# Seven rounds of a state-space scan: X and Y turned by VectorE blocks and transfers in place of TensorE, and TensorE's slab wait split in two

## The reference

```python
h = h + 0.5 * _swiglu(_rmsnorm(h, ffn1_norm[l]), ...)
h = h + _mixer(_rmsnorm(h, mix_norm[l]), ...)       # three mixers, gated and summed
h = h + 0.5 * _swiglu(_rmsnorm(h, ffn2_norm[l]), ...)
return _rmsnorm(h, final_norm)
```

```python
xbc = jax.nn.silu(_causal_conv(_in_cols(u, w_in, 6), ssm_conv_w, ssm_conv_b))
xs_, bm, cm = jnp.split(xbc, [SSM_D_INNER, SSM_D_INNER + SSM_GROUPS * SSM_DSTATE], axis=-1)
...
def step(state, inp):
    xc, bc, cc, dtc, dac = inp
    cum = jnp.cumsum(dac, axis=1)
    seg = cum[:, :, None] - cum[:, None, :]
    decay = jnp.exp(jnp.where(mask, seg, -jnp.inf))
    cb = jnp.einsum('btgn,bsgn->btsg', cc, bc)
    xdt = xc * dtc[..., None]
    y = jnp.einsum('btsg,btsgr,bsgrp->btgrp', cb, decay, xdt)
    y = y + jnp.einsum('btgn,bgrpn->btgrp', cc, state) * jnp.exp(cum)[..., None]
    to_end = jnp.exp(cum[:, -1:] - cum)
    state = jnp.exp(cum[:, -1])[..., None, None] * state + jnp.einsum('bsgn,bsgrp->bgrpn', bc, xdt * to_end[..., None])
    return state, y
...
y = y.reshape(bsz, seq, SSM_D_INNER) * jax.nn.silu(z.astype(F32))
y = _rmsnorm(y.reshape(bsz, seq, SSM_GROUPS, SSM_D_INNER // SSM_GROUPS),
             ssm_norm.reshape(SSM_GROUPS, SSM_D_INNER // SSM_GROUPS))
y_ssm = y.reshape(bsz, seq, SSM_D_INNER).astype(u.dtype) @ w_branch_ssm
```

## Time and profile before

| | us |
|---|---|
| median of three runs | 1797.28 |
| the three runs | 1797.56, 1797.28, 1795.0 |
| profiled execution | 1794.89 |
| its span in the trace | 1793.1 |

### The profile page before, as it was taken

How to read it: one execution, slowest core, us unless ns; L and a number is a source line. 1 busy time by engine, 2 the same in 40 slices (tenths; PEclk the granted TensorE clock), 3 DMA queues, 4 the chain that set the end, 5 groups by cost and what they waited for, 6 DMA issues and landing times.

```text
span 1793.1 us, 26524 instructions
## 1 busy us (share of the span) xinstructions
PE 1784.8 (100%) x10012; PEld 1504.1 (84%) x10012; DVE 959.2 (53%) x1393; ACT 633.3 (35%) x1002; POOL 89.0 (5%) x92
## 2 busy tenths in 40 slices
PE   9999999999999999999999999999999999999998
PEld 7888888888888888888988888888888888888887
DVE  5444443369988888623544445665334544444333
ACT  5222322244544445422333344443222332222221
POOL 2111100000000000000000000000000011111000
PEclk9999999999999999999999999999999999999999
DMA  5333323334233332232222323322333332233332
GB/s 172 105 94 100 98 94 105 105 96 94 83 94 88 87 95 84 69 106 94 95 71 71 94 82 93 93 90 74 94 98 99 96 94 94 94 96 102 106 105 71
DMA packets 53937, 169.30 MB, mean 94 GB/s; under 512 B 6336, under 2 KB 13760, under 8 KB 53872
## 3 DMA queue, kind: packets, MB, share of 16 engines
q1 hardware_dynamic: 45824, 159.15, 27.9%
q10 hardware_dynamic: 8048, 9.24, 2.7%
HBM read 166.21 MB, written 2.16 MB: 94 GB/s over the span
## 4 chain that ended last, share of the span: by engine, by line
PE 95%; DVE 3%; ACT 1%; issue 1%; DMA 0%; ACTq 0%; DVEq 0%; SPq 0%
PE G L547 48%; PE I L547 16%; PE G L614 11%; PE G L567 8%; PE I L1050 1%; PE I L1026 1%; PE I L1016 1%; PE G L874 1%; PE I L674 1%; PE I L811 1%; PE I L820 1%; DVE CV L1936 1%; PE I L830 1%; DVE WL L1673 1%; PE I L986 0%
## 5 line engine op out<-in xcount | busy, mean ns | idle before, releaser
L1673 DVE TENSOR_TENSOR WL<-RAW,WH 128x1024 fp32r<-128x1024 f32 x296 | 372.1, 1260 | 290.0 <-ACT WH L1147 280.8
L1147 ACT CAST WH<-RAW 128x1024 fp32r<-128x1024 f32 x295 | 306.4, 1046 | 225.2 <-PE I L547 125.9
L547 PE MATMUL G<-UH,WH 128*128 128x512 f32 x664 | 164.2, 389 | 0.0
L547 PE MATMUL G<-UH,WL 128*128 128x512 f32 x664 | 164.0, 389 | 0.0
L547 PE MATMUL G<-UL,WH 128*128 128x512 f32 x664 | 163.9, 389 | 0.0
L547 PEld LDWEIGHTS G<-UL,WH 128*128 128x128 f32 x664 | 124.6, 188 | 25.9
L547 PEld LDWEIGHTS G<-UH,WL 128*128 128x128 f32 x664 | 124.6, 188 | 25.9
L547 PEld LDWEIGHTS G<-UH,WH 128*128 128x128 f32 x664 | 124.5, 188 | 25.9
L547 PE MATMUL G<-NH,WH 128*128 128x512 f32 x448 | 113.5, 395 | 0.0
L547 PE MATMUL G<-NL,WH 128*128 128x512 f32 x448 | 110.8, 389 | 0.0
L547 PE MATMUL G<-NH,WL 128*128 128x512 f32 x448 | 110.7, 389 | 0.0
(11 more groups left out here) (352 smaller groups left out, 2619.3 us busy)
## 6 DMA issues: line engine op xcount, KB each, us to landing
RAW<-in_slabs SPq DMA_DIRECT2D x296, 512.0 KB, 3.5
cum_rows<-kept_rows ACTq DMA_DIRECT2D x16, 256.0 KB, 6.8
bias<-in_rel ACTq DMA_DIRECT2D x16, 128.0 KB, 2.8
bias<-in_rel ACTq DMA_DIRECT2D x16, 112.0 KB, 2.8
h<-in_x SPq DMA_DIRECT2D x6, 256.0 KB, 5.7
out_y<-h SPq DMA_DIRECT2D x4, 256.0 KB, 2.2
h<-in_x ACTq DMA_DIRECT2D x2, 256.0 KB, 3.6
out_y<-h ACTq DMA_DIRECT2D x4, 128.0 KB, 1.8
```

What stands on the lines that cost most here:

```text
L547: ins = mm(dst, slab(W, n)[:, (k - k0) * P:(k - k0 + 1) * P], R[:, k, :], start=begin and which == 0 and k == k0, stop=end and which == 2 ...
L1147: nc.scalar.copy(slab(WH, n), RAW[:, n.slot, :]).then_inc(split_hi, 1)
L1673: V.tensor_tensor(slab(WL, n), RAW[:, n.slot, :], slab(WH, n).bitcast(F32), ALU.subtract).then_inc(split_lo, 1)
```

## The change

Three things change.

1. X of groups 1 to 7 (`turn_x`, `move_x`): DVE turns the 32 x 32 blocks of XT in place of TensorE (two `transpose` instructions of 128 x 512 float32 each round, put between `lo(n+5)` and silu 2), and SP moves the blocks to their partitions with 16 transfers of 32 partitions x 8 pieces of 128 bytes (32 KB each). ACT's XD and DVE's XTE and XDT then read `x_tokens` in SBUF. Group 0 is still turned by TensorE.
2. Y of groups 0 to 6 (`turn_y`, `move_y`): two more DVE transposes of 128 x 512 behind `ssm_scale`, 16 more transfers in two parts with a slab's load between them. `ssm_hi` and `ssm_lo` read the result from SBUF (SU, which lies where SL lies). `ssm_hi` moves to ACT's t = 3, `ssm_lo` and `group_gain` to the end of DVE's round, and in the stage behind the rounds both move behind `lo(n+5)`. Group 7 is still turned by TensorE.
3. TensorE waits for the rounded slab (`need_hi`) ahead of a slab's first matmul and for its remainder only ahead of the last third. The second state update no longer waits for `ssm_hi` and `ssm_lo`; new waits for `ssm_lo` stand ahead of the products that read SH and SL.

The buffers lie in places that are free at the time. The diff, cut to its core:

```diff
+            def move_x(g):
+                sp.wait_ge(x_blocks, g)
+                for b in range(4):
+                    for q in range(4):
+                        sp.dma_start(x_tokens[32 * q:32 * q + 32, :, :].rearrange("p j (f c) -> p (j f) c", f=2)[:, :, 32 * b:32 * b + 32],
+                                     x_turned[32 * b:32 * b + 32, :, 32 * q:32 * q + 32]).then_inc(x_moved, 16)
...
+            def move_y(g, parts):
+                sp.wait_ge(y_blocks, g + 1)
+                for b in parts:
+                    for q in range(4):
+                        sp.dma_start(SU[32 * q:32 * q + 32, bass.ds(2 * g, 2), :].rearrange("p f (j c) -> p (f j) c", c=P)[:, :, 32 * b:32 * b + 32],
+                                     y_turned[32 * b:32 * b + 32, :, 32 * q:32 * q + 32]).then_inc(y_moved, 16)
...
+            ahead = N_SSM + 15
+            loads(RING, ahead)
+            move_x(1)
+            next_load(At(ahead))
+            move_y(0, (0, 1))
+            next_load(At(ahead + 1))
+            move_y(0, (2, 3))
+            with sp.Fori(0, NG - 2) as i:
+                for j in range(2, 6):
+                    next_load(At(ahead + j, i, 6))
+                move_x(i + 2)
+                next_load(At(ahead + 6, i, 6))
+                move_y(i + 1, (0, 1))
+                next_load(At(ahead + 7, i, 6))
+                move_y(i + 1, (2, 3))
+            loads(ahead + 6 * (NG - 2) + 2, N_SLABS)
...
             def fm(dst, n, RH, RL):
+                need_hi(n)
+                blocks(dst, n, 0, KT, RH, RL, True, False, (0, 1))
                 need_slab(n)
-                blocks(dst, n, 0, KT, RH, RL, True, True).then_inc(slab_done, 1)
+                ins = blocks(dst, n, 0, KT, RH, RL, False, True, (2,))
+                ins.then_inc(slab_done, 1)
...
-                for j in range(TT):
-                    for f in range(2):
-                        nc.tensor.transpose(I01[:, j * 256 + f * P:j * 256 + (f + 1) * P],
-                                            XT[:, f, j * P:(j + 1) * P], ident[:])
+                if isinstance(g, int) and g == 0:
+                    for j in range(TT):
+                        for f in range(2):
+                            nc.tensor.transpose(I01[:, j * 256 + f * P:j * 256 + (f + 1) * P],
+                                                XT[:, f, j * P:(j + 1) * P], ident[:])
...
-                pe.wait_ge(sems["ssm_hi"], last("ssm_hi", g - 1))
-                pe.wait_ge(sems["ssm_lo"], last("ssm_lo", g - 1))
...
-                    0: lambda: (ssm_turn(i), ssm_turn_back(i - 1)), 1: lambda: ssm_cb_u(i),
+                    0: lambda: ssm_turn(i), 1: lambda: ssm_cb_u(i),
...
             ssm_turn(g)
-            ssm_turn_back(g - 1)
+            pe.wait_ge(sems["ssm_lo"], last("ssm_lo", 3))
             output_half(n + 1, wn + 1, 0, (0, 1))
...
             need_slab(n + 4)
+            pe.wait_ge(sems["ssm_lo"], last("ssm_lo", NG - 2))
             output_part(n + 4, wn + 1, KT, 2 * KT - 2, SH, SL, False, False)
...
+            def turn_y(g):
+                dve.wait_ge(sems["ssm_scaled"], last("ssm_scaled", g))
+                dve.wait_ge(sems["ssm_scaled_act"], last("ssm_scaled_act", g))
+                if not isinstance(g, int) or g > 0:
+                    dve.wait_ge(y_moved, 256 * g)
+                for f in range(2):
+                    ins = V.transpose(y_turned[:, TT * f:TT * f + TT, :], Y[:, :, f * P:(f + 1) * P])
+                ins.then_inc(y_blocks, 1)
+            def turn_x(g):
+                dve.wait_ge(sems["conv_done"], after("conv_done", g, 1))
+                dve.wait_ge(x_moved, 256 * (g - 1))
+                dve.wait_ge(sems["x_copied"], after("x_copied", g - 1))
+                for f in range(2):
+                    ins = V.transpose(x_turned.rearrange("p (j f) c -> p f j c", f=2)[:, f, :, :],
+                                      XT[:, f, :].rearrange("p (j c) -> p j c", c=P))
+                ins.then_inc(x_blocks, 1)
...
                     if t == 0 and not first:
                         ssm_x(inner)
-                        ssm_lo(inner - 1)
-                        group_gain(inner)
                     if t != 2 or not first:
                         lo(n + t + 3)
+                    if t == 2:
+                        turn_x(p)
...
                     ssm_scale(inner)
+                turn_y(inner)
                 z_silu(p, wn + 4)
                 lo(n + 7)
                 group_scalars(p)
                 lo(n + 8)
+                if not first:
+                    ssm_lo(inner - 1)
+                    group_gain(inner)
```

More of the change, by code:

```diff
@@ L417, in _, with next_load @@
                 sp.dma_start(wgk_raw[32 * k:32 * k + 16, :], a["wgk"]).then_inc(wgk_landed, 16)
[L418 to L425, removed]
+            def next_load(n):
+                sp.wait_ge(split_lo, n.value - (RING - 1))
+                load(n)
@@ new lines, in move_x, with loads @@
+            def move_x(g):
[4 more added lines that the diff above has]
+                                     x_turned[32 * b:32 * b + 32, :, 32 * q:32 * q + 32]).then_inc(x_moved, 16)
+            def loads(begin, end):
+                whole = -(-begin // RING)
+                for n in range(begin, whole * RING):
+                    next_load(At(n))
+                with sp.Fori(whole, end // RING) as i:
+                    for j in range(RING):
+                        next_load(At(j, i, RING))
+                for n in range(end // RING * RING, end):
+                    next_load(At(n))
@@ L612, in tm_tile @@
                         if j == 0 and which == 0 and k == 4:
+                            need_hi(n + 1)
+                        if j == 0 and which == 2 and k == 0:
+                            need_slab(n)
+                        if j == 0 and which == 2 and k == 4:
                             need_slab(n + 1)
@@ L1925, in ssm_lo, with ssm_lo_last @@
                 dve.wait_ge(sems["group_gain"], after("group_gain", g))
[L1926 removed]
+                dve.wait_ge(y_moved, 256 * (g + 1))
+                for f in range(2):
+                    dve.wait_ge(sems["ssm_hi"], after("ssm_hi", g, f))
+                    inc(V.scalar_tensor_tensor(tile_of(SL, 2 * g + f), tile_of(SU, 2 * g + f), ssm_norm_cols[f],
+                                               tile_of(SH, 2 * g + f).bitcast(F32), ALU.mult, ALU.subtract), "ssm_lo")
+            def ssm_lo_last():
+                dve.wait_ge(sems["group_gain"], after("group_gain", NG - 1))
+                evict_lo(I34, SH, SL, 2 * NG - 2, ssm_norm_cols, "ssm_hi", NG - 1, "ssm_lo")
+            def turn_y(g):
[3 more added lines that the diff above has]
+                    dve.wait_ge(y_moved, 256 * g)
+                for f in range(2):
+                    ins = V.transpose(y_turned[:, TT * f:TT * f + TT, :], Y[:, :, f * P:(f + 1) * P])
+                ins.then_inc(y_blocks, 1)
             taps_n = [0]
@@ L1972, in ssm_x @@
             def ssm_x(g):
-                dve.wait_ge(sems["x_copied"], after("x_copied", g))
-                inc(V.tensor_tensor(XTE[:].rearrange("p j (r c) -> p (j r) c", c=CH), heads(I01[:]), rows(2),
+                if isinstance(g, int) and g == 0:
+                    source = heads(I01[:])
+                    dve.wait_ge(sems["x_copied"], after("x_copied", g))
+                else:
+                    source = x_tokens.rearrange("p j (r c) -> p (j r) c", c=CH)
+                    dve.wait_ge(x_moved, 256 * g)
+                dve.wait_ge(sems["u_done"], last("u_done", g - 1))
+                inc(V.tensor_tensor(XTE[:].rearrange("p j (r c) -> p (j r) c", c=CH), source, rows(2),
                                     ALU.mult), "xte_ready")
                 dve.wait_ge(sems["intra_done"], last("intra_done", g - 1))
-                inc(V.tensor_tensor(XDT[:].rearrange("p j (r c) -> p (j r) c", c=CH), heads(I01[:]), rows(1),
+                inc(V.tensor_tensor(XDT[:].rearrange("p j (r c) -> p (j r) c", c=CH), source, rows(1),
                                     ALU.mult), "xdt_ready")
+            def turn_x(g):
+                dve.wait_ge(sems["conv_done"], after("conv_done", g, 1))
+                dve.wait_ge(x_moved, 256 * (g - 1))
+                dve.wait_ge(sems["x_copied"], after("x_copied", g - 1))
+                for f in range(2):
+                    ins = V.transpose(x_turned.rearrange("p (j f) c -> p f j c", f=2)[:, f, :, :],
+                                      XT[:, f, :].rearrange("p (j c) -> p j c", c=P))
+                ins.then_inc(x_blocks, 1)
             def ssm_cb(g):
@@ L2182, in _ @@
             lo(n + 5)
+            ssm_lo(g - 1)
+            group_gain(g)
             ssm_scale(g)
-            ssm_lo(g)
+            ssm_lo_last()
             lo(n + 6)
```

55 lines of the change are left out of this document (44 added, 11 removed).

## The result

| | before | after |
|---|---|---|
| median, 20 runs each | 1794.91 us (1794.36 to 1797.56) | 1799.09 us (1797.96 to 1799.99) |
| ratio, 95% interval | 1 | 1.0022 (1.0016 to 1.0028) |
| span of the profiled execution | 1793.1 us | 1796.4 us |
| busy PE, DVE | 1784.8, 959.2 us | 1777.4, 976.9 us |
| five looped rounds, `gconv` to `gconv` | 208.48 us | 213.68 us |

The change makes the kernel slower by 4.2 us, just over the 3.6 us that I had called the limit of what can be told. The forecast was -0.7 us. By the spans it is +3.3 us where the sum had -0.7: 4.0 us to explain.

What follows compares the result with a forecast made beforehand. PE bound the rounds at 42.18 us; afterwards DVE's chain would, at 41.91. The update starts 1.4 us earlier, a new wait returns 0.7: net -0.7 us, 1796.6 us against the median of 1797.28; range 1793 to 1806.5.

Steps and rivals of the forecast that it cites:

- PE sets the rounds now, DVE's chain of 40.83 us is next: Looped rounds: PE takes 42.18 us without a gap; the chain of DVE and ACT is only 1.35 us under it.
- Rival (c): DVE's chain has slack read as fixed, so PE sets the rounds again: 1786.4 us, in part 1792; chance 0.12.
- The price of a block transpose, t = 0.60: Each DVE transpose of 512 float32 per partition takes 0.60 us, one element per cycle and lane.
- (a): DVE's transposes are slow: at t = 1.14 the time is 1807.8 us; chance 0.20, mostly nearer 0.9.
- (b): DVE's transposes run at the double rate, t = 0.40: 2.8 us less, 1793.8; chance 0.07.
- `turn_x` in full on the chain, `turn_y` in the wait of `z_silu`: DVE's rounds: turn_x adds 1.20 us in seven rounds; turn_y costs nothing up to t of about 0.88.
- Transfers and split waits cost nothing: SP's moves are hidden up to about 0.85 us an issue; TensorE's two waits per slab win and lose nothing.
- (d): SP's issues exceed 0.85 us or queued loads come late; at 1.0 us an issue +17, 1813 us; chance 0.06.
- (e): Small transfer pieces choke the DMA engines: +56 us in each of seven rounds, near 2190 us; chance 0.02.
- `ssm_lo`, moved behind `lo(n+8)`, stays on the chain: Late in DVE's looped round: the moved passes stay on the chain, with 0.12 us back in each looped round.
- read from SBUF its two passes cost 1.28 against 1.40: ssm_lo on DVE: two passes cost 2 x 0.60 + 0.08 from SBUF against 1.40, 0.12 us back each looped round.
- PE's clock: PE's granted clock stays full if waits of 2.7 us leave it so; a fall would add to the slow side.

Runs made afterwards that it cites:

- Y alone, mended: Changed kernel with X turned by TensorE again, ssm_lo and group_gain moved earlier in loop and stage behind, ssm_hi(6) earlier behind the loop: 1788.61 us, ratio 0.9968.
- X alone: Changed kernel with Y turned by TensorE again and ssm_hi, ssm_lo, group_gain back at their old places; only X moved: 1795.75 us, ratio 1.0004.
- the run of the split waits alone: Kernel before with only the split waits for rounded parts and remainders added: 1794.54 us, ratio 0.9998.
- the mended order: Whole change with ssm_lo and group_gain ahead of group_scalars and lo(n + 8), reordered stage behind, 5 added matmuls a round: 1795.49 us, ratio 1.0003.
- Y alone: Changed kernel with X turned by TensorE again in all rounds; only Y by VectorE's blocks and transfers: 1790.86 us, ratio 0.9978 to before.
- the run with added matmuls: Changed kernel with 5 more unused 128 x 128 matmuls on TensorE each round, ahead of the products of B and C: 1798.17 us, ratio 1.0018 to before.

## Why the prediction was wrong

Its structure held and its sum was short by 4.0 us of span, enough to turn a small gain into a loss. The step that failed is the price of moving `ssm_lo` and `group_gain` to the end of the loop's body: the sum put it at 0.12 us back in each looped round, and the trace shows 0.47 to 0.52 us of new idle time a round, ahead of `gconv`, and nothing back. A second cost, the falls of TensorE's clock, was named and put at nothing.

The forecast's 1796.6 us stand nearer to the measured 1799.09 than the sum deserves. They rest on a median of three, 1797.28; over 20 runs it is 1794.91, from which the same sum gives 1794.2, and the miss is 4.9 us. Two smaller sums don't come out either: by PE's side, 11.6 us less 2.7 + 5 x 1.4 + 1.0 + 0.7 leaves a gain of 0.2 us and not 0.7, and t from 0.53 to 0.72 at 14 us for each microsecond gives 1795.6 to 1798.3. Point by point:

- **PE sets the rounds now, DVE's chain of 40.83 us is next:** right, and seen bare in the 40.84 us of Y alone, mended. Rival (c), slack in that chain, falls.
- **The price of a block transpose, t = 0.60:** right. Two of them, once for X and once for Y:

```profile
442.24 1.30 DVE L2097 STREAM_TRANSPOSE x_turned<-XT 128x512 f32<-128x512 f32 x2
...
539.59 1.30 DVE L2030 STREAM_TRANSPOSE y_turned<-Y 128x512 f32<-128x512 f32 x2 [0.23 <-DVE Y L2153]
```

  A pair is recorded at 1.30 us; in the stream of the chain the next pass starts 1.22 us behind the pair's start (483.91 to 485.13), 0.61 each. Rivals (a) and (b) fall. The Trainium skill (VectorE: DVE Perf Modes, The three transpose paths) gives 311 ns for 128 bf16 columns; the estimate of four times that, 1.24 us, would have been twice what was measured. The advice that the prediction quotes from that page, TensorE where PSUM will do, came true for X and not for Y.
- **`turn_x` in full on the chain, `turn_y` in the wait of `z_silu`:** right, by X alone (42.0 us in the rounds behind the disturbed two) and by Y alone, mended (nothing added to 40.83).
- **Transfers and split waits cost nothing:** right for X's transfers and for the waits, by their runs, and for Y's by the 40.84 us of Y alone, mended. SP's issues took 0.65 us each for X (16 in about 10.4) and 0.72 for Y (8 in 5.8), over the 0.5 that I took and under the 0.85 from which it would matter. The prediction's own sign of trouble, WH waiting for its load, did show once: 1.76 us at 469.01, in the round behind the first moves (before has no such wait there). That round is as long as round 4, which has none (43.00 and 42.99 us), so it cost nothing that can be told. Rivals (d) and (e) fall; the engines' time for q1 rose from 27.9% to 29.9% of the span, for 60928 more packets: 16 x (0.299 x 1796.4 - 0.279 x 1793.1) us over 60928 is about 10 ns each (12 with the 27.4% that q1 takes in the run of the split waits alone), against the 18 that I took.
- **"`ssm_lo`, moved behind `lo(n+8)`, stays on the chain": the step that failed.** I priced its two passes and not its place. It moved the long pass away from the end of the loop's body, and with that uncovered the turn of the loop: 2.4 us of idle time in five rounds, 1.87 us of which the mended order gets back. The price was not to be seen in the trace of before as idle time, since there a 1.2 us pass ran over it.
- **"read from SBUF its two passes cost 1.28 against 1.40": wrong.** 1.41 us. Five times 0.12 is 0.6 us. The premise was unfounded in the rows of before too: `z_silu`, which reads PSUM, does its two passes in 1.28 there, so it was not PSUM that made `ssm_lo` longer; what does stays open. The Trainium skill (VectorE: DVE Perf Modes, The TRN2 errata, its table of cycles by placement) has a VectorE instruction that reads SBUF 62 cycles cheaper than one that reads PSUM; for this two-operand pass, with the other operand in SBUF already, the rows show no difference.
- **PE's clock:** named and not priced. It fell in two of five rounds behind waits of 1.9 us, and cost 0.86 us. A wait that is a gain in the sum is not free. PE's busy time fell by 7.4 us and not by some 11; the trace has the state updates behind the falls busy for longer, but I didn't account for the whole difference.
- **The new wait for SL in the stage behind:** right, 0.80 us against 0.7, at the product that stood at 737.74:

```profile
740.90 1.63 PE L940 MATMUL G<-SH,WH 128*128 128x512 f32 x6 [0.80 <-DVE SL L2015]
```

Together, as the trace of after has them: 2.4 + 0.6 + 0.86 = 3.9 of the 213.68 - 5 x 41.91 = 4.1 us by which the rounds are too long. What is left, 0.05 us a round, is the size of what I had rounded away (0.61 for 0.60 among it). The mends gave back 0.86 and 1.87 us of it, 2.7; the rest, 210.95 - 209.55 = 1.4 us, is the 0.6 of `ssm_lo` and the 0.8 by which `group_gain`'s copy waits longer in the mended order. The 0.6 is read from the rows; no run took it out. The rounds' excess less 0.35 us by which round 2 began earlier than reckoned gives most of the 4.0; about 0.2 us behind the rounds I did not trace.

Why X and Y together are worse than each: Y alone is 3.8 us faster, X alone 1.05 slower (nothing in its executions at the full clock), and both 4.2 slower where the sum of the two would be 2.8 faster. A round is the longer of PE's work and DVE's chain. Y takes 0.79 us from PE and puts nothing on a chain that has 1.35 us to spare; that uses up more than half of the distance, and the 0.5 to 0.6 us at the turn of the loop use up the rest. X's 1.22 us then lengthen a round that the chain already sets, and its 0.87 us off PE are worth nothing.

## What to carry to other kernels

Read the order of the engine that is next in line as a chain of its own, as here, and then price a moved step by its place too: which instruction becomes the last of a loop's body, and what it hid. Keep a pass of a microsecond there. When a change moves work from one engine to another, test its parts alone: of two moves of the same size one was worth 6 us with the order put right. The other was worth nothing alone and lost 6.9 us beside the first, since only one of them fell into an existing wait.

## What the hardware showed that I had not expected

- VectorE at the turn of its loop: 0.47 to 0.52 us of idle time with a 0.17 us instruction ahead of it (0.58 to 0.88 in Y alone), none seen behind a pass of 1.2 us.
- TensorE's granted clock fell to its lower level behind waits of 1.89 to 1.92 us in some rounds and not in others of the same kernel and length (467.75 and 553.37 against 638.91); behind waits of 0.60 us it did not fall in six rounds of the run with added matmuls. What decides among the equal waits stays open.
- Two of `ssm_lo`'s passes over 512 float32, with a scalar and two tensors, are recorded at 1.40 us with the first operand in PSUM and at 1.41 with it in SBUF.
